# A hybrid decoder trunk on one core: the order of the 512-column and 256-column matmuls within a unit of a weight-stationary product

## The reference

```python
h = x @ w_in                                   # 2048 x 8336, split into the parts of the mixers
m = concat(a_out, b_out, c_out) @ w_out        # 2048 x 2048
x = layer_norm(ALPHA * x + m, ln1_g, ln1_b)
hdn = jnp.square(jax.nn.relu(x @ w_up))        # 2048 x 8192
x = layer_norm(ALPHA * x + hdn @ w_down, ln2_g, ln2_b)
```

## Time and profile before

| | |
|---|---|
| median of three runs | 2513.42 us |
| the profiled execution | 2510.86 us |
| its span, first to last instruction | 2509.2 us |
| TensorE matmul busy | 2455.9 us, 98% |
| TensorE weight load busy | 2101.0 us, 84% |
| VectorE busy | 1497.7 us, 60% |
| ScalarE busy | 1118.5 us, 45% |
| mean granted TensorE clock | 0.99 |
| read from HBM | 452.33 MB, 182 GB/s with the writes |

### The profile page before, as it was taken

One profiled execution on the slowest core, in us unless ns is written; L12 is line 12 of the kernel. 1 busy time (PEld: TensorE's weight loads), 2 busy tenths in 40 slices (PEclk: granted clock), 3 DMA queues, 4 the chain that ended last, 5 costly groups with the idle time before them and its releaser, 6 DMA issues.

```text
span 2509.2 us, 35620 instructions
## 1 busy us (share of the span) xinstructions
PE 2455.9 (98%) x12808; PEld 2101.0 (84%) x12808; DVE 1497.7 (60%) x1960; ACT 1118.5 (45%) x1493; POOL 69.1 (3%) x84
## 2 busy tenths in 40 slices
PE   8999999999999999999899999999999999999997
PEld 7888888878888888888788888888788888888886
DVE  5575666566556556556656756665665565565655
ACT  4444444344345344344334444543453443443443
POOL 2000000020000000000100000000200000000001
PEclk9999999999999999999989999999999999999999
DMA  8455555645665555555354555456456656556552
GB/s 281 161 191 168 169 168 168 217 168 187 201 189 196 187 191 194 191 194 187 104 183 165 174 168 177 161 170 227 171 176 200 195 186 199 185 189 197 185 197 89
DMA packets 229559, 458.31 MB, mean 183 GB/s; under 512 B 7280, under 2 KB 12144, under 8 KB 228240
## 3 DMA queue, kind: packets, MB, share of 16 engines
q1 hardware_dynamic: 225504, 441.74, 53.3%
q0 software_dynamic: 1616, 11.14, 1.2%
q10 hardware_dynamic: 2272, 3.15, 0.4%
HBM read 452.33 MB, written 3.67 MB: 182 GB/s over the span
## 4 chain that ended last, share of the span: by engine, by line
PE 94%; DVE 3%; issue 1%; DMA 1%; ACT 1%; POOL 0%; SPq 0%; DVEq 0%; ACTq 0%; POOLq 0%
PE pw L459 33%; PE pw L463 16%; PE pw L481 14%; PE pw L482 14%; PE pw L483 14%; PE pa L527 1%; DMA raw<-in_w_in_dram 1%; PE pa L603 1%; DVE y L978 1%; DVE w_lo L898 1%; PE pa L524 0%; PE pa L500 0%; DVE y L984 0%; PE pa L611 0%; ACT w_hi L696 0%
## 5 line engine op out<-in xcount | busy, mean ns | idle before, releaser
L898 DVE TENSOR_TENSOR w_lo<-raw,w_hi 128x1024 fp32r<-128x1024 f32 (+1 forms) x848 | 1022.4, 1221 | 749.1 <-ACT w_hi L696 736.2
L696 ACT ACTIVATE w_hi<-raw 128x1024 fp32r<-128x1024 f32 (+1 forms) x848 | 877.3, 1047 | 1059.6 <-PE pw L483 569.7
L459 PE MATMUL pw<-act_a,w_hi 128*128 128x512 f32 x3584 | 1132.1, 397 | 4.3 <-DVE w_lo L898 4.3
L463 PEld LDWEIGHTS pw<-act_a,w_lo 128*128 128x128 f32 x3584 | 674.4, 188 | 159.4
L463 PE MATMUL pw<-act_a,w_lo 128*128 128x256 f32 x3584 | 705.2, 278 | 0.0
L459 PEld LDWEIGHTS pw<-act_a,w_hi 128*128 128x128 f32 x3584 | 548.8, 189 | 6.8 <-DVE w_lo L898 4.7
L481 PE MATMUL pw<-w_hi,act_b 128*128 128x512 f32 x1280 | 498.6, 390 | 0.1
L482 PE MATMUL pw<-w_lo,act_b 128*128 128x512 f32 x1280 | 498.0, 389 | 0.0
L483 PE MATMUL pw<-w_hi,act_b 128*128 128x512 f32 x1280 | 498.0, 389 | 0.0
L481 PEld LDWEIGHTS pw<-w_hi,act_b 128*128 128x128 f32 x1280 | 240.3, 188 | 50.3 <-issue 0.9
L483 PEld LDWEIGHTS pw<-w_hi,act_b 128*128 128x128 f32 x1280 | 240.3, 188 | 50.0
(11 more groups left out here) (129 smaller groups left out, 865.9 us busy)
## 6 DMA issues: line engine op xcount, KB each, us to landing
raw<-in_w_in_dram SPq DMA_DIRECT2D x128, 1024.0 KB, 5.0
raw<-in_w_up_dram SPq DMA_DIRECT2D x128, 1024.0 KB, 5.3
raw<-in_w_down_dram SPq DMA_DIRECT2D x128, 1024.0 KB, 5.1
raw<-in_w_out_dram SPq DMA_DIRECT2D x32, 1024.0 KB, 5.1
work<-in_ln_g_dram POOLq DMA_DIRECT2D x4, 1024.0 KB, 4.9
work<-in_ln_b_dram POOLq DMA_DIRECT2D x4, 1024.0 KB, 8.0
raw<-in_w_in_dram SPq DMA_DIRECT2D x8, 288.0 KB, 7.6
out_dram<-y SPq DMA_DIRECT2D x4, 512.0 KB, 2.8
```

The lines of the kernel that those rows point to most:

```text
L459: nc.tensor.matmul(pw[:, b, :], w_hi[:, slot + i, cols], act_a[:, k].rearrange("p a t -> p (a t)"), start=(k == 0), stop=False)
L463: last = nc.tensor.matmul(pw[:, b, SEQ:2 * SEQ], w_lo[:, slot + i, cols], act_a[:, k, 0, :], start=False, stop=(k == KT - 1))
L696: nc.scalar.activation(w_hi[:, slot:slot + PAIR, 0:width], raw[:, PAIR * u:PAIR * (u + 1), 0:width], ACT.Copy) \
L898: V.tensor_tensor(w_lo[:, slot:slot + PAIR, 0:width], raw[:, PAIR * u:PAIR * (u + 1), 0:width], w_hi[:, slot:slot + PAIR, 0:width].bitcast ...
```

## The change

In every unit of a feature chunk but the last one of the chunk, the two kinds of matmul are no longer alternated bank by bank: first come all eight matmuls with `w_hi` (two for each of the four banks), then all eight with `w_lo`. In unit 0 the four waits for `bank_free` stay ahead of each bank's first matmul, so they now stand among the eight first ones. Unit 7 of each chunk keeps its order, with `bank_full` raised after each bank. The number of matmuls, their operands and the sums are the same. The wait for `lo_ready`, and the matmul that raises `unit_free` (the last of the unit), keep their places.

```diff
-                for n, b in enumerate(BANKS[c]):
-                    if u == 0:
-
-                        pe.wait_ge(bank_free[b], now.value(USES[c][b] + 1, U_L[b], U_Q[b]))
-                    cols = slice(n * P, (n + 1) * P)
+                def with_hi(n, b):
                     for i in range(PAIR):
                         k = PAIR * u + i
-                        nc.tensor.matmul(pw[:, b, :], w_hi[:, slot + i, cols], act_a[:, k].rearrange("p a t -> p (a t)"),
-                                         start=(k == 0), stop=False)
+                        nc.tensor.matmul(pw[:, b, :], w_hi[:, slot + i, n * P:(n + 1) * P],
+                                         act_a[:, k].rearrange("p a t -> p (a t)"), start=(k == 0), stop=False)
+
+                def with_lo(n, b):
                     for i in range(PAIR):
                         k = PAIR * u + i
-                        last = nc.tensor.matmul(pw[:, b, SEQ:2 * SEQ], w_lo[:, slot + i, cols], act_a[:, k, 0, :],
+                        last = nc.tensor.matmul(pw[:, b, SEQ:2 * SEQ], w_lo[:, slot + i, n * P:(n + 1) * P], act_a[:, k, 0, :],
                                                 start=False, stop=(k == KT - 1))
-                    if u == UNITS - 1:
-                        last.then_inc(bank_full[b], 1)
+                    return last
+
                 if u < UNITS - 1:
+                    for n, b in enumerate(BANKS[c]):
+                        if u == 0:
+
+                            pe.wait_ge(bank_free[b], now.value(USES[c][b] + 1, U_L[b], U_Q[b]))
+                        with_hi(n, b)
+                    for n, b in enumerate(BANKS[c]):
+                        last = with_lo(n, b)
                     last.then_inc(unit_free, 1)
+                else:
+                    for n, b in enumerate(BANKS[c]):
+                        with_hi(n, b)
+                        with_lo(n, b).then_inc(bank_full[b], 1)
```

## The result

The changed kernel takes 2522.63 us (median of 10 runs, 2519.22 to 2529.86) against 2514.55 us for the kernel before on the same chip (10 runs). The ratio is 1.0033, 95% interval 1.0018 to 1.0048: 8.3 us slower, 4.5 to 12. The forecast was 1.0 us faster; the time lies inside the range of 2497 to 2527, the direction is wrong.

What follows compares the result with a forecast made beforehand. TensorE, busy 98% of the span, was taken as the bound. Pace -3.9 us, bank waits +2.9 and unit end 0 gave -1.0 us, from the median 2513.42 to 2512.4; eight-in-ten range 2497 to 2527.

Steps and rivals of the forecast that it cites:

- The price of an L: A 256-column w_lo matmul in a run costs 120.0 ns: its columns plus a fixed 13.3 ns per matmul with its load.
- Rival 1: Faster: surplus goes with columns, a 256-column matmul costs 113.3 ns, mixing widths costs 16.7 ns a group; 2499 us, chance 0.30.
- rival 2: Slower: loads and full-rate streams hinder each other in w_lo runs, 125 ns per 256-column matmul; 2527 us, chance 0.18.
- rival 3: Order tells nothing: a 256-column matmul stays 121.7 ns, no pace gained, only bank waits cost; 2516.3 us, chance 0.12.
- The two places that gave 128 ns for an L: Upper bound for a 256-column matmul: first ones of successive chunks (1061.42 to 1062.13), and last ones before a token chunk (175.54).
- The price of a change of kind: Changing between 512- and 256-column matmuls and back costs 3.3 ns; one pair a unit instead of four, 392 units, -3.9 us.
- the 2790 that the prediction had set as a sign of being wrong: Length of a changed unit: forecast 2.777 us, called wrong if under 2.765 or above 2.790 us.
- The halts: Unit 0 of second to fourth MLP chunks: TensorE waits for the last bank, 24 times 0.12 us, +2.9 us; other chunks nothing.
- The end of a unit: The unit's last matmul still frees its slots, ScalarE's split starts at the same place, DMAs keep theirs; no cost.

Runs made afterwards that it cites:

- turned runs: Kernel before, with units 1 to 6 grouped by kind, odd units w_lo first, even units w_hi first, giving runs of 16 of a kind; ratio 1.0000 (0.9989 to 1.0012).

## Why the prediction was wrong

**The price of an L, right.** L = 120.0 ns in a run, forecast 120.0, from a surplus that goes with the matmul and not with the columns. Rival 1's premise (113.3) and rival 2's (125) both fell, the second although the kernel did get slower, and so did rival 3's (121.7), which had the sign by its halts alone. The two places that gave 128 ns for an L were read wrongly: the trace has L of 118 and 120 ns at the first and of 113 and 119 at the second, and what was left over was the lateness of the H beside them.

**The price of a change of kind, the step that failed.** "The new unit has one such pair of changes instead of four" is true, but its price of 3.3 ns was read from pairs of H, and it isn't the price of a pair around eight: that is 19.7 ns, and the unit takes 2793 ns, past the 2790 that the prediction had set as a sign of being wrong. Behind an L the H are late by some 6, 9, 1, 6 and 4 ns, 27 in all, and the first two L of a run start 7 and 1 ns early. In H H L L each return is cut off after two H, and the L gain their 8 back at once; a run of eight H pays in full, 27 less 8, 19.7 ns by the unit. The term was -3.9 us (10 ns less in 392 units) and is +2.5 (6.5 ns more; +2.1 measured in units 1 to 6). Both numbers were on the table: the earlier trace rows showed the 27 ns, and the prediction used them in rival 1 alone, with an L of 113.3. With an L of 120 the same sum gives 8 x 226.7 + 8 x 120 + 27 - 8 = 2793, the measured unit.

**The halts, right.** 24 waits, forecast 24, all in the second to fourth MLP chunk of a quarter; unit 0 is 0.10 to 0.13 us longer there, forecast 0.12; +2.8 us in the run with unit 0 alone, forecast +2.9. The projections' banks cost nothing, with their last one free at 1.04 us, and the banks behind token chunks neither.

**The end of a unit, right for the steady work.** No split is late.

**What was left out.** The sum took the clock for granted. The rest of the span holds the norms, which the change doesn't touch, and the time at 1.2 GHz was longer in every profile of the change (66.8 to 74.2 us) than in any of before (53.9 to 61.9); over all executions the difference is 6 us, worth some 3 by the estimate above. Of the median's 8 us the steady units are 5.1; the 3 that remain would lie there. What in the new order lengthens that time is not settled.

So the sign hangs on one term: with the right price of a pair the sum would have been +2.5 + 2.9 = +5.4 us, 2518.8, against 2522.63 measured. The size lacks the 3 us as well.

The turned runs would be the version to beat both, with 1.2 us less in the steady units than before; at 1.0000 (0.9989 to 1.0012) that can't be told from no change.

## What to carry to other kernels

When matmuls of different widths with a load each are mixed, sum the starts over a whole period and over the way back into the steady pace; the price of a change between them is not the same for runs of two as for runs of eight, it can differ between two places of one execution (2773 and 2827 ns for the same H L H L), and a rival's number has to be tried in the forecast's own sum. When an order gathers first uses of buffers in front, compare each one's new due time, load included, with when the last reader frees it, bank by bank: that gave 24 halts of 0.12 us from one row. A saving or loss of a few us has to be read in the part of the trace that repeats to 0.1 us, since the pauses and the clock move more than that from one execution to the next; and what a few profiles say of the clock is held against the granted clock of all executions.

## What the runs showed of the hardware that I had not expected

An fp32r matmul with its own load costs 13.3 ns over its columns' time at 2.4 GHz, whether it streams 512 or 256 columns (226.7 and 120.0 ns in a run); with 384 columns the eight of a run take 173 to 185 ns, 177 on average, 17 over the columns' 160.

The H behind a run of L are late for five matmuls, 27 ns in all, the same behind 8, 10 and 16 L in the change and in the turned runs, and behind two L at 11 of the 16 changes to a token chunk in the trace of before (at the other five it is 11 ns over two H). A pair of changes costs 3.4 ns between pairs of each, 17 between fours, 19.7 between eights. Alternating H and L has two paces in one execution, 2773 and 2827 ns a unit, 0 and 6.7 ns a pair, and each holds until something else comes between the matmuls.

A load released by VectorE after a wait of 0.26 us delayed TensorE by only 0.10 to 0.13 us, since the matmul before it was still streaming for the rest of it.
